# Channel LayerNorm statistics as one row through small DMAs, with the two sums side by side, and the Conformer convolutions two at a time

## The reference

```python
def hybrid_layer(x, w_in, conv_a_w, ..., w_out, ln_g, ln_b):
    h = jnp.einsum("btd,de->bte", x, w_in)                        # (B, T, D_IN)
    a_bg, a_cg, a_v, a_z, b_v, b_g, b_z, c_u, c_z = jnp.split(h, splits, axis=-1)
    y_a = a_bg * causal_depthwise_conv(a_cg * a_v, conv_a_w, conv_a_b)      # 3 taps
    y_a = y_a * jax.nn.silu(a_z)
    u_b = b_v * jax.nn.sigmoid(b_g)
    u_b = causal_depthwise_conv(u_b, conv_b_w, conv_b_b)                    # 31 taps
    u_b = jax.nn.silu(layer_norm(u_b, ln_b_g, ln_b_b))                      # over the 512 channels
    y_b = u_b * jax.nn.silu(b_z)
    p = multiscale_causal_pool(c_u)
    p = jnp.einsum("btgc,gcd->btgd", p, pool_w) + pool_b
    y_c = p.reshape(bsz, t, W_C) * pool_scale * jax.nn.silu(c_z)
    out = jnp.einsum("bte,ed->btd", jnp.concatenate([y_a, y_b, y_c], axis=-1), w_out)
    return layer_norm(DEEPNORM_ALPHA * x + out, ln_g, ln_b)
```

## Time and profile before

| | us |
|---|---|
| median of 3 runs | 790.82 (790.62 to 790.99) |
| the profiled execution, its own time | 790.98 |
| its span on the slowest core (first to last instruction) | 789.4 |
| spans of the 8 cores | 787.3 to 789.4 |
| granted TensorE clock, mean of each core | 0.993 to 0.996 |

### The profile page before, as it was taken

The page is one execution under the profiler, slowest core; times in us unless marked ns, Lnnn a source line. Parts: engine busy times, 40 slices in busy tenths (PEclk is TensorE's granted clock), DMA queues, the critical chain, the costliest instruction groups (busy, mean ns, idle before and its releaser), DMA issues.

```text
span 789.4 us, 16350 instructions; the slowest of 8 cores (787.3 to 789.4 us)
## 1 busy us (share of the span) xinstructions
PE 767.9 (97%) x5215; PEld 408.5 (52%) x5269; DVE 484.1 (61%) x769; ACT 380.0 (48%) x631; POOL 306.6 (39%) x379
## 2 busy tenths in 40 slices
PE   8899999999999999999999999999999999999994
PEld 7556666654444444445555566666444444444441
DVE  1322268986656577455655657975665654887467
ACT  1222367555545584354454478546433447635421
POOL 4121148864011146346111016945501113783393
PEclk9999999999999999999999999999999999999998
DMA  8877889987987864654797895994646677342022
GB/s 123 162 152 144 177 136 167 149 129 176 212 209 188 186 138 62 94 70 82 129 213 179 180 216 103 154 174 72 133 112 178 159 194 187 54 67 28 1 99 115
DMA packets 77060, 108.59 MB, mean 138 GB/s; under 512 B 24496, under 2 KB 46000, under 8 KB 76464
## 3 DMA queue, kind: packets, MB, share of 16 engines
q0 software_dynamic: 28944, 61.22, 46.5%
q1 hardware_dynamic: 48032, 46.31, 22.2%
HBM read 116.78 MB, written 16.78 MB: 169 GB/s over the span
## 4 chain that ended last, share of the span: by engine, by line
PE 92%; issue 3%; DMA 2%; DVE 2%; POOL 0%; ACT 0%; DVEq 0%; ACTq 0%; POOLq 0%
PE ps L556 60%; PE ps L1135 20%; PE ps L709 8%; DMA xT<-xint 2%; PE ps L753 1%; PE ps L739 1%; PE ps L948 1%; DVE mem L591 1%; DVE xT L591 1%; DVE mem L928 0%; DVE mem L586 0%; PE ps L537 0%; ACT mem L582 0%; POOL wrg L497 0%; PE ps L1058 0%
## 5 line engine op out<-in xcount | busy, mean ns | idle before, releaser
L556 PE MATMUL ps<-xT,wrg 128*128 128x512 bf16 (+7 forms) x2790 | 515.4, 339 | 3.7 <-issue 1.4
L556 PEld LDWEIGHTS ps<-xT,wrg 128*128 128x128 bf16 x2816 | 272.1, 98 | 229.7 <-issue 13.7
L582 ACT ACTIVATE mem<-ps 128x512 f32<-128x512 f32 (+12 forms) x284 | 131.3, 484 | 181.1 <-PE ps L556 140.4
L586 POOL TENSOR_TENSOR yb<-mem 128x512 bf16<-128x512 f32 (+3 forms) x120 | 129.0, 1081 | 130.4 <-ACT mem L582 57.8
L1135 PE MATMUL ps<-wo,yb 128*128 128x512 bf16 x743 | 174.7, 379 | 1.1
L497 POOL DMA_DIRECT2D wrg<-w_in_r x144 | 80.4, 561 | 204.0 <-PE ps L556 131.2
L582 ACT ACT_TABLE_LOAD x72 | 92.4, 1283 | 62.8 <-DVE mv L1173 46.5
L1135 PEld LDWEIGHTS ps<-wo,yb 128*128 128x128 bf16 x768 | 75.0, 98 | 86.3 <-issue 0.7
L582 ACT ACTIVATE mem<-mem,par 128x384 f32<-128x384 f32 (+3 forms) x80 | 57.4, 727 | 70.1 <-DVE mem L586 62.2
L591 DVE SCALAR_TENSOR_TENSOR Rb<-Rb,ps 128x512 f32<-128x512 f32 (+1 forms) x59 | 40.2, 681 | 73.2 <-PE ps L1135 72.3
L591 DVE SCALAR_TENSOR_TENSOR mem<-mem,par 128x384 f32<-128x384 f32 (+3 forms) x80 | 66.0, 826 | 14.5 <-ACT mem L582 10.1
(11 more groups left out here) (70 smaller groups left out, 383.4 us busy)
## 6 DMA issues: line engine op xcount, KB each, us to landing
wrg<-w_in_r POOLq DMA_DIRECT2D x144, 256.0 KB, 5.5
mem<-mem SPq DMA_DIRECT2D x64, 135.0 KB, 3.2
Rb<-xin SPq DMA_DIRECT2D x16, 512.0 KB, 5.1
x1s<-Rb POOLq DMA_DIRECT2D x16, 512.0 KB, 4.5
Rb<-x1s SPq DMA_DIRECT2D x13, 512.0 KB, 5.0
mem<-mem SPq DMA_DIRECT2D x64, 103.0 KB, 4.9
wo<-w_out_r POOLq DMA_DIRECT2D x24, 256.0 KB, 9.0
out<-Rb POOLq DMA_DIRECT2D x8, 512.0 KB, 3.3
```

The source lines that it names most:

```text
L556: o = P.add("pe", lambda e, kk=kk: e.matmul(bk.ap[:, 0:N], lhsT=wrg_t[:, s, kk, :], rhs=xT(kk, tok0, N), start=(kk == 0), stop=(kk == 7)), ...
L582: return P.add("act", lambda e: e.activation(out=out, in_=in_, func=func, **kw), reads=reads, writes=writes, cost=cost).fin
L586: return P.add(eng, lambda e: e.tensor_tensor(out=out, in0=in0, in1=in1, op=op), reads=reads, writes=writes, cost=0.15 + n * (0.0022 if en ...
```

## The change

It has three parts.

- **Statistics as one row.** The two sums go to one bank, with 32 columns of ones each and side by side: the sum of `cb` on partitions 0 to 31, of the squares on 32 to 63. All four squares are made first (two of them in space of the `X` buffers). ScalarE copies the bank's 64 partitions to `m`. Two SyncE DMAs spread one row of each sum over r partitions with k values each (`ty`, N = r x k; k is 4, 3, 3, 2 for N = 512, 384, 288, 256). Variance (2 operations), square root and reciprocal are done on that small tile. Two DMAs write mean and reciprocal to DRAM (`ln_d`), and two read them back as 128 equal rows into `m` and `rs`.
- **Convolutions two at a time.** Convolutions of a unit are numbered n = group x tiles + tile. One with an even n is held back until n + 1 is due, then both take a bank and their 64 matmuls are issued back to back. In units of two tiles the two of group 3 stay single.
- **Refitted estimates.** The costs of several operations are changed, none of which changes an instruction.

The small hunks on estimates stand first, without context, the rest in full.

```diff
@@ -309,6 +309,7 @@
+    ln_d = nc.dram_tensor("lnrows", [4, 2, 512], F32, kind="Internal").ap()
@@ -369,6 +370,7 @@
+        ty_t = sb("tiny", [128, 4, 3, 4], F32)
@@ -391,6 +393,7 @@
+        R_ty, R_lm, R_ln = [mk("ty%d_" % i, 2) for i in range(4)], mk("lm", 4), mk("ln", 4)
@@ -571,6 +574,8 @@
+            if bias is not None and n > 1:
+                cost += 0.08 + (0.08 if scale is not None else 0.0)
@@ -581,21 +586,21 @@
-        def tt(eng, out, in0, in1, op, reads, writes, psum=False):
+        def tt(eng, out, in0, in1, op, reads, writes, psum=False, more=0.0):
-                         cost=0.15 + n * (0.0022 if eng == "pool" else 0.00106), port=not psum).fin
-
-        def stt(out, in0, scalar, in1, op0, op1, reads, writes, psum=False):
+                         cost=0.15 + n * ((0.0022 if eng == "pool" else 0.00106) + more), port=not psum).fin
+
+        def stt(out, in0, scalar, in1, op0, op1, reads, writes, psum=False, more=0.0):
-                         reads=reads, writes=writes, cost=0.15 + n * 0.00106, port=not psum).fin
+                         reads=reads, writes=writes, cost=0.15 + n * (0.00106 + more), port=not psum).fin
-            return P.add(eng, lambda e: e.tensor_copy(out=out, in_=in_), reads=reads, writes=writes, cost=0.25, port=True).fin
+            return P.add(eng, lambda e: e.tensor_copy(out=out, in_=in_), reads=reads, writes=writes, cost=0.4, port=True).fin
-            P.add(eng, lambda e: e.memset(out, 0.0), writes=writes, cost=0.1)
+            P.add(eng, lambda e: e.memset(out, 0.0), writes=writes, cost=0.25)
...
@@ -699,21 +704,46 @@
             spawn(fz, gz())
             p2fill()
 
+        first = {}
+
         def conv(u, g, t, off, N, d, Ub, Uv, last):
             li, blk = UNITS[u]
             q = 4 * u + g
             yield lambda: diags[0] > q
-            Pc = yield from new_bank()
-            for j in range(8):
-                for s4 in range(4):
-                    o = P.add("pe", lambda e, j=j, s4=s4: e.matmul(
-                        Pc.ap[32 * s4:32 * s4 + 32, 0:N], lhsT=Lm_t[:, q % 2, s4, j, :], rhs=Uv[:, s4, d + 4 * j:d + 4 * j + N],
-                        start=(j == 0), stop=(j == 7), tile_position=(0, 32 * s4)),
-                        reads=[R_Lm[q % 2], Ub.res[s4]], writes=Pc.res if (j, s4) in ((0, 0), (7, 3)) else [], cost=mmc(N) / 4)
-            Ub.free()
+            job = {}
+
+            def emit():
+                Pc = job["bank"]
+                for j in range(8):
+                    for s4 in range(4):
+                        o = P.add("pe", lambda e, j=j, s4=s4: e.matmul(
+                            Pc.ap[32 * s4:32 * s4 + 32, 0:N], lhsT=Lm_t[:, q % 2, s4, j, :], rhs=Uv[:, s4, d + 4 * j:d + 4 * j + N],
+                            start=(j == 0), stop=(j == 7), tile_position=(0, 32 * s4)),
+                            reads=[R_Lm[q % 2], Ub.res[s4]], writes=Pc.res if (j, s4) in ((0, 0), (7, 3)) else [],
+                            cost=mmc(N) / 4 + (0.1 if (j, s4) in ((0, 0), (7, 3)) else 0.0))
+                Ub.free()
+                job["fin"] = o.fin
+
+            nt = len(unit_tiles(li, blk))
+            n = g * nt + t
+            alone = nt == 2 and g == 3
+            if n % 2 == 0 and not alone:
+                first[u, n] = job, emit
+                yield lambda: "fin" in job
+            else:
+                if not alone:
+                    yield lambda: (u, n - 1) in first
+                    pj, pe = first.pop((u, n - 1))
+                    pj["bank"] = yield from new_bank()
+                    job["bank"] = yield from new_bank()
+                    pe()
+                else:
+                    job["bank"] = yield from new_bank()
+                emit()
+            Pc, fin = job["bank"], job["fin"]
             if last:
-                spawn(o.fin + 1.0, call(lambda: emit_diag(q + 2)))
-            yield o.fin
+                spawn(fin + 1.0, call(lambda: emit_diag(q + 2)))
+            yield fin
             cb = yield from take(Z_CB + (g * TBH + off) * 2, BF16, N)
             f = act(cb.ap, Pc.ap[:, 0:N], AF.Identity, Pc.res + [R_par[li]], cb.res, scale=0.5, bias=pcol(li, g, 4), psum=True)
             Pc.free()
@@ -732,47 +762,66 @@
             sqb = {}
 
             def square(g):
-                sqb[g] = yield from take(Z_SQ + 1024 * rot("sq", 2), BF16, N)
+                sqb[g] = yield from take((Z_SQ, Z_SQ + 1024, Z_X + 2048, Z_X + 3072)[g], BF16, N)
                 return act(sqb[g].ap, cbs[g].ap, AF.Square, cbs[g].res, sqb[g].res)
 
-            def sqmm(g):
-                o = P.add("pe", lambda e: e.matmul(Pq.ap[:, 0:N], lhsT=ones_t[:], rhs=sqb[g].ap, start=(g == 0), stop=(g == 3)),
-                          reads=[R_ones] + sqb[g].res, writes=Pq.res if g in (0, 3) else [], cost=mmc(N))
+            def sums(g):
+                for i, x in enumerate((cbs[g], sqb[g])):
+                    o = P.add("pe", lambda e, i=i, x=x: e.matmul(
+                        Ps.ap[32 * i:32 * i + 32, 0:N], lhsT=ones_t[:, 32 * i:32 * i + 32], rhs=x.ap, start=(g == 0), stop=(g == 3),
+                        tile_position=(0, 32 * i)), reads=[R_ones] + x.res, writes=Ps.res if (g, i) in ((0, 0), (3, 1)) else [],
+                        cost=mmc(N) / 2 + 0.015 + (0.1 if (g, i) in ((0, 0), (3, 1)) else 0.0))
                 sqb[g].free()
                 return o.fin
 
             yield lnb_free
             lnb_busy[0] = True
-            yield from square(0)
-            f = yield from square(1)
+            for g in range(4):
+                f = yield from square(g)
             yield f + 1.5
-            yield lambda: spare(2)
             Ps = yield from new_bank()
-            Pq = yield from new_bank()
             for g in range(4):
-                o = P.add("pe", lambda e, g=g: e.matmul(Ps.ap[:, 0:N], lhsT=ones_t[:], rhs=cbs[g].ap, start=(g == 0), stop=(g == 3)),
-                          reads=[R_ones] + cbs[g].res, writes=Ps.res if g in (0, 3) else [], cost=mmc(N))
-            sqmm(0)
-            f = sqmm(1)
-            yield f
-            act(m.ap, Ps.ap[:, 0:N], AF.Copy, Ps.res, m.res, scale=1.0 / 512, psum=True)
-            act(rs.ap, Ps.ap[:, 0:N], AF.Square, Ps.res, rs.res, scale=1.0 / 512, psum=True)
-            Ps.free()
-            yield from square(2)
-            f = yield from square(3)
-            yield f + 1.5
-            sqmm(2)
-            f = sqmm(3)
+                f = sums(g)
             lnb_busy[0] = False
             yield f
-            f = stt(rs.ap, Pq.ap[:, 0:N], 1.0 / 512, rs.ap, ALU.mult, ALU.subtract, Pq.res + rs.res, rs.res, psum=True)
-            Pq.free()
+            f = act(m.ap[0:64], Ps.ap[0:64, 0:N], AF.Copy, Ps.res, m.res, scale=1.0 / 512, psum=True)
+            Ps.free()
+            yield f + 0.3
+            yield lambda: len(ln_free) > 0
+            il = ln_free.pop(0)
+            k = {512: 4, 384: 3, 288: 3, 256: 2}[N]
+            r = N // k
+            ty, Ry = ty_t[0:r, il, :, 0:k], R_ty[il]
+            for i in range(2):
+                row = m.ap[32 * i:32 * i + 1, 0:N]
+                row = bass.AP(row.tensor, row.offset, [row.ap[0], [k, r], [1, k]])
+                o = P.add("sp", lambda e, i=i, row=row: e.dma_start(out=ty[:, i], in_=row), reads=m.res, writes=[Ry[i]], dma=True,
+                          cost=0.6, land=0.3)
+            yield o.fin + 1.0
+
+            def small(fn, reads, writes):
+                return P.add("dve", fn, reads=reads, writes=writes, cost=0.15).fin
+            small(lambda e: e.tensor_tensor(out=ty[:, 2], in0=ty[:, 0], in1=ty[:, 0], op=ALU.mult), Ry[:1], Ry[1:])
+            f = small(lambda e: e.tensor_tensor(out=ty[:, 1], in0=ty[:, 1], in1=ty[:, 2], op=ALU.subtract), Ry[1:], Ry[1:])
             yield f
-            f = act(rs.ap, rs.ap, AF.Sqrt, rs.res + [R_eps], rs.res, bias=eps_t[:, 0:1])
+            f = act(ty[:, 2], ty[:, 1], AF.Sqrt, Ry[1:] + [R_eps], Ry[1:], bias=eps_t[0:r, 0:1])
             yield f
-            f = P.add("dve", lambda e: e.reciprocal(out=rs.ap, in_=rs.ap), reads=rs.res, writes=rs.res, cost=0.1 + 0.0064 * N).fin
+            f = small(lambda e: e.reciprocal(out=ty[:, 1], in_=ty[:, 2]), Ry[1:], Ry[1:])
+            yield f + 0.3
+            for i in range(2):
+                row = ln_d[il, i, 0:N].rearrange("(p c) -> p c", c=k)
+                o = P.add("sp", lambda e, i=i, row=row: e.dma_start(out=row, in_=ty[:, i]), reads=[Ry[i]], writes=[R_ln[il]] if i else [R_lm[il]],
+                          dma=True, cost=0.6, land=0.3)
+            yield o.fin + 1.0
+            for i, x in enumerate((m, rs)):
+                row = ln_d[il, i, 0:N]
+                row = bass.AP(row.tensor, row.offset, [[0, 128], [1, N]])
+                o = P.add("sp", lambda e, x=x, row=row: e.dma_start(out=x.ap, in_=row), reads=[R_lm[il], R_ln[il]][i:i + 1], writes=x.res,
+                          dma=True, cost=0.6, land=1.0)
+            ln_free.append(il)
```

(8 more changed lines are left out.)

## The result

The changed kernel takes 849.93 us (847.75 to 855.39, 4 runs) against 790.74: 1.0755 times the time before, 95% interval 1.071 to 1.0801. The forecast was 782.7 with a range of 780.3 to 788.0, and 0.10 for slower. It is 59 us slower. Some executions on these chips were disturbed and much longer; every time and ratio in this document leaves them out, and e9 and e11, of which one execution was left, have no ratio.

What follows compares the result with a forecast made beforehand. PE was taken to bound the kernel from about 24 us to the last matmul. Profiled 790.98 - 4.0 (pairs) - 4.8 (sums) + 0.7 (waits, order) = 782.9, hence 782.7 for the median; range 780.3 to 788.0.

Steps and rivals of the forecast that it cites:

- The excursion per change of shape: On PE, convolutions: 0.22 us paid per switch to 32-column matmuls and back; pairing removes 18 of 40, saving 4.0 us.
- Two sums side by side: On PE, LayerNorm sums: two column tiles run at the price of one, saving 4.8 us over ten tiles.
- DVE's relief worth nothing: On DVE: dropping wide reciprocals removes 27 us of work, worth nothing at the end since PE had no wait on these.
- I price hops of median length at nothing: Six added SyncE DMAs per tile: hops landing in time, up to 3.1 us after the issue's end, cost PE nothing.
- the nearest row: Ub copies taken as model for a hop's landing: median 3.5 us from issue start, 2.9 after its end, in time.
- the share of 0.87: First unit: DMA engines 87% busy, cited for small DMAs coming late.
- 4.4 us covered: DVE's longest hold by ScalarE, taken as the part of a late hop's delay that costs PE nothing.
- The slower rival: Small DMAs come late and DVE stands: PE loses 1.6 us per tile, 16 in all, about 799 us; chance 0.10.
- break-even of 8.9 us: Hop length at which PE loses 0.8 us per tile, cancelling the change's 8.1 us gain.
- The order: All new waits and reordering together: +0.7 us, between -2.3 and, hops apart, about +3; refitted costs change no instruction.
- The range's lower end: 780.3 us, described as the forecast with PE's 2.3 us of body waits won back and no stall.
- The Trainium skill's rule against the change: DMA transfers below 512 B miss line rate; for 8 to 16 B pieces, said to feed only the rival with late DMAs.

Runs made afterwards that it cites:

- e9: Kernel before plus, per tile, two spreading DMAs and two small DRAM writes waiting for them, read by no engine: 812.06 us, a single measurement.
- e11: Changed kernel with old costs and consumers 4, 4 and 6 us after the hops, pieces still 8 to 16 B: 836.53 us, a single measurement.
- e1: Kernel before with the paired convolutions alone, LayerNorm and costs as before: 787.9 us, ratio 0.9957.
- e5: Changed kernel without hops and with old costs: pairs and side by side sums, wide variance, root and reciprocal, statistics incorrect: 782.15 us, ratio 0.9883.
- e7: Kernel before with the six hop DMAs added per tile, chained 12 us apart, into tiles nobody reads: 818.06 us, ratio 1.033.
- e16: Kernel before plus two spreads and two DRAM writes per tile, the writes from a constant tile and waiting for no spread: 807.03 us, ratio 1.0196.
- e13: Kernel before with only the two spreading DMAs added per tile, read by no engine: 794.22 us, ratio 1.0039.
- e4: Changed kernel with what waits for each hop placed 12 us after its estimated end, not 1, 1 and 2: 830.68 us, ratio 1.0506.
- e3: Changed kernel with its convolutions single again, keeping row statistics and refitted costs: 828.92 us, ratio 1.0479.
- e2: Kernel before with the refitted costs alone, which alter only the order of instructions: 796.4 us, ratio 1.0073.
- e10: Kernel before with only two broadcasts from DRAM added per tile, read by no engine: 795.8 us, ratio 1.0057.
- e14: Kernel before with only two small-piece DRAM writes added per tile, from a constant tile, waiting for nothing: 795.89 us, ratio 1.0067.

## Why the prediction was wrong

- **The excursion per change of shape: right.** 2.72 us for a pair, the weight side's idle 22 times and not 40, 3.4 of 4.0 us in e1. "TensorEngine Tiling (Array Packing)" in the Trainium skill, section Tiling Modes, had it so, and the pair's row agrees.
- **Two sums side by side: right**, 5.7 us measured for 4.8.
- **DVE's relief worth nothing: right.** With DVE as busy as before (490 us) and no hops, e5 meets the forecast time.
- **"I price hops of median length at nothing": the step that failed**, in three ways. First, the nearest row: I took the Ub copies' 3.5 us and set aside the small loads' 8.9 and 9.7 as standing in the head. That was a misreading: each of those rows holds two loads, and only one of the two was issued in the head (at 7.0 and 7.9 us). The other was issued at 92.1 and at 92.7 us, in the first unit, and landed after 8.0 and 7.7 us. The Ub copies had a median of 4.5 us in that unit from 60 us on, and none was issued there after 90.7 us, so they said nothing of the stretch where the hops stand. In the first unit the hops landed at medians of 9.7, 11.0 and 13.0. I had the share of 0.87 in hand and used it only for the rival. It is a mean over 153 us; from 125 to 150 us it was 0.98.
- Second, **a hop was taken as something that only waits**. It also slows others, for which the sum had no term. With no consumer at all (e7) it is 26 us, with weight loads at a median of 23.6 us in place of 8.8, and the DRAM writes in the full stretch make 12.4 us by themselves (e16 against e13). In the changed kernel itself PE's waits for weights are only 5.1 us, since PE mostly stands for DVE there; the slowed transfers show in its hops.
- Third, **cover was taken from an unlike wait, and for one hop of three**. "4.4 us covered" came from one hold of DVE by ScalarE; in the changed kernel holds of 6.8 and 9.2 us follow within 12 us, and ScalarE and GpSimd are held with DVE. Both the main sum and the rival worked out a loss only for the first hop, for which DVE waited 17.8 us; for the third, DVE waited 38.3 and GpSimd 55.1. A stall then brings the lower clock: 17 of the 69 us lost.
- **The slower rival had part of the mechanism and the wrong size**: 799 for 850, and a chance of 0.10. The first unit's medians lie above its break-even of 8.9 us. With all consumers moved back (e4) some 20 us return, near its 16, and 40 stay. What was missing in its price was the traffic, the second and third hop, the clock, and the pairs beside the hops (e3).
- **The order: mis-sized.** I took +0.7 us and bounded it, hops apart, at about +3; e2 measures +5.8.
- **The range's lower end** does not follow from its own words: with 2.3 us won back in place of 0.7 lost it is 779.7, not 780.3. That decides nothing here.
- **An expectation's figure**: the two broadcasts add 4.2 MB (112.82 against 108.59 MB on the pages of e10 and before), not the 3.4 that e10's expectation says.
- **The Trainium skill's rule against the change**: "DMA: Bandwidth & Descriptors", section Specifications, puts line rate at 512 B and more. I wrote that it would feed the rival and not the sum. The runs agree with the rule's direction, and it should have moved the chance: 96 to 128 pieces of 8 to 16 B against 16 of 64 to 128 B is 1.0755 against 1.0183. That the cause is a read-modify-write, as the page has it, no run here shows. The runs also tell the two kinds apart, which that rule does not: pieces of 8 to 16 B from SBUF to SBUF left the weight loads' pieces at 207 to 212 ns, those to DRAM in the same stretch came with 283 to 292.

## What to carry to other kernels

Before a chain of small DMAs goes into in-order lists, read the DMA share of the very stretch it will stand in, and take landing times from rows issued in that stretch: look up when each row was issued. In a full stretch count pieces as well as bytes, those written to DRAM above all, and price what they take from the transfers that feed the bottleneck. Count every hop of a chain. Cut a row into as few pieces as the small operation allows, and test the DMAs alone, into tiles that nobody reads, before the consumers are built on them; then check in the trace that they stand where they would in the change (in e14 they did not). An edit that pays on PE alone (pairs, side by side sums) should be timed without its companion: here each was right to 1 us.

## What the runs showed of the hardware that I had not expected

- Small writes to DRAM lower what full DMA engines move. From 125 to 150 us: 150 GB/s before, 168 with spreads, 122 with spreads and writes, 111 with all six, 141 in the change with 16 larger pieces, at shares of 0.98 to 1.07. A 2048 B piece of other transfers took 283 to 292 ns with the writes there and 207 to 212 without.
- How long a weight load takes to land and what it costs are two things: a median of 19.2 us with 0.2 us of waits for weights at the projections (e10), 22.4 us with 6.9 (e16).
- A stall of several us costs more than itself: in the changed kernel the granted clock is 0.80 over 25 us in which PE was busy for 16.6.
